# Twelve modulation vectors fetched or summed at other outputs in a fused two-block kernel

## The reference, cut to what matters

```python
mod = silu(c) @ w_ada + b_ada            # [1, 3072] a layer
shift, scale, gate = split(mod, 3)
h = rms_norm(x, g) * (1 + scale) + shift
x = x + gate * mixer(h)                  # the MLPs: x + 0.5 * gate * swiglu(h)
swiglu(x) = (silu(a) * b) @ w_down       # a, b = halves of x @ w_up
```

## Time and profile before

| | us |
|---|---|
| median of 3 runs | 1373.81 (1369.03 to 1379.53) |
| the profiled execution | 1375.45 |
| its span | 1373.7 |
| TensorE busy | 1204.4 (88%) |
| VectorE busy | 877.5 (64%) |
| DMA over the span | 160 GB/s |

### The profile page before, as it was taken

The page is one execution under the profiler, slowest core; times in us unless marked ns, Lnnn a source line. Parts: engine busy times, 40 slices in busy tenths (PEclk is TensorE's granted clock), DMA queues, the critical chain, the costliest instruction groups (busy, mean ns, idle before and its releaser), DMA issues. The chain is left out here.

```text
span 1373.7 us, 19952 instructions
## 1 busy us (share of the span) xinstructions
PE 1204.4 (88%) x7677; PEld 998.7 (73%) x7677; DVE 877.5 (64%) x1432; ACT 543.4 (40%) x962; POOL 286.1 (21%) x160
## 2 busy tenths in 40 slices
PE   4878896988896889999999878999798989999997
PEld 4665575766675667887877666889797967788886
DVE  4773697379856447865556785687556555555554
ACT  1232365242246353344453335334324243544443
POOL 0012042125421222441113323110313111000001
PEclk9989898899888799999999989789898989999999
DMA  7877155147745246976634335389000034555552
GB/s 267 282 244 230 62 184 169 62 155 262 241 138 170 92 138 219 323 225 199 192 118 152 112 123 154 120 261 338 1 4 2 4 102 143 169 184 184 184 169 76
DMA packets 143481, 221.62 MB, mean 161 GB/s; under 512 B 10823, under 2 KB 66715, under 8 KB 143259
## 3 DMA queue, kind: packets, MB, share of 16 engines
q1 hardware_dynamic: 140512, 216.37, 48.7%
q10 hardware_dynamic: 2875, 3.98, 0.8%
HBM read 219.27 MB, written 1.05 MB: 160 GB/s over the span
## 5 line engine op out<-in xcount | busy, mean ns | idle before, releaser
L532 PE MATMUL bank<-w_parts,lhs_hi 128*128 128x512 f32 (+2 forms) x960 | 399.3, 416 | 30.3 <-ACT w_parts L486 28.3
L486 ACT CAST w_parts<-ring 128x1024 fp32r<-128x1024 f32 (+2 forms) x288 | 288.7, 1032 | 280.3 <-PE bank L534 89.4
L534 PE MATMUL bank<-w_parts,lhs_lo 128*128 128x512 f32 (+2 forms) x960 | 391.7, 408 | 0.0
L491 DVE TENSOR_TENSOR w_parts<-ring,w_parts 128x1024 fp32r<-128x1024 f32 (+2 forms) x224 | 299.7, 1364 | 130.0 <-ACT w_parts L486 126.3
L547 PE MATMUL bank<-w_parts,lhs_hi 128*128 128x512 f32 (+2 forms) x960 | 276.2, 403 | 11.5 <-DVE w_parts L491 11.5
L532 PEld LDWEIGHTS bank<-w_parts,lhs_hi 128*128 128x128 f32 x960 | 191.3, 199 | 73.1 <-ACT w_parts L486 24.9
L491 POOL TENSOR_TENSOR w_parts<-ring,w_parts 128x1024 fp32r<-128x1024 f32 (+1 forms) x64 | 165.9, 2595 | 324.3 <-ACT w_parts L486 316.0
L547 PEld LDWEIGHTS bank<-w_parts,lhs_hi 128*128 128x128 f32 x960 | 183.5, 195 | 55.1 <-DVE w_parts L491 17.1
L534 PEld LDWEIGHTS bank<-w_parts,lhs_lo 128*128 128x128 f32 x960 | 191.0, 199 | 37.8
L662 DVE SCALAR_TENSOR_TENSOR ada_acc<-ring,c_act,ada_acc 128x512 f32<-128x512 f32 x203 | 176.6, 870 | 13.0 <-DMA ring<-in_ada_w 2.7
L609 PE MATMUL bank<-const,arena 128*128 128x128 f32 (+2 forms) x322 | 60.0, 340 | 34.9 <-DVE arena L1633 7.2
(11 more groups left out here) (347 smaller groups left out, 1531.2 us busy)
## 6 DMA issues: line engine op xcount, KB each, us to landing
ring<-in_w_ffn_up SPq DMA_DIRECT2D x176, 256.0 KB, 3.9
ring<-in_w_ada SPq DMA_DIRECT2D x72, 512.0 KB, 4.7
ring<-in_ada_w SPq DMA_DIRECT2D x48, 512.0 KB, 4.6
ring<-in_w_ffn_down SPq DMA_DIRECT2D x44, 512.0 KB, 4.4
ring<-in_w_in SPq DMA_DIRECT2D x44, 512.0 KB, 4.0
ring<-in_dil_w_in SPq DMA_DIRECT2D x32, 512.0 KB, 4.2
ring<-in_nsa_w_in SPq DMA_DIRECT2D x20, 512.0 KB, 4.6
ring<-in_w_in SPq DMA_DIRECT2D x20, 416.0 KB, 4.2
```

The costliest lines, as they stand in the source:

```text
L486: eng.copy(hi, raw).then_inc(hi_ready, 1)
L491: eng.tensor_tensor(lo, raw, hi.bitcast(F32), ALU.subtract).then_inc(lo_ready[who], 1)
L532: pe.matmul(b, x_hi, w, start=(k0 + k == 0), stop=False)
L534: mm = pe.matmul(b, x_lo, w, start=False, stop=False)
```

## The change

The vectors move down the stream:

| stage | before: vector after output | after |
|---|---|---|
| dilated | 12 to 16 after 1 to 5 | 12 to 15 after 1 to 4 |
| beside the attention | 17, 18 | 16, 17 |
| first MLP | 19 to 23 after 2 to 6 | 18 to 23 after 2 to 7 |
| z, gate outputs | 24, 25 after z; 26 to 29 after gate 0 to 3 | 24, 25 after z; 26, 27 after gate 0, 1 |
| last MLP | none | 28, 29 after 1, 2 |

TensorE's sums: in the dilated projections `ada_sum(10+j)` after output j (j = 2 to 5), so one output later than the fetch; 24 to 27 after z 1 and gate 0 to 2, also one later; in the first MLP 16+j after output j (j = 0 to 7), in the last 28 and 29 after outputs 1 and 2. From vector 12 on, the stream collects one vector less when it begins one.

```diff
+FFN1_ADAS = {j: 16 + j for j in range(8)}
+FFN2_ADAS = {1: 28, 2: 29}
 # first_stages
-        if j:
+        if 1 <= j < 5:
             s.append(ada(11 + j))
-    s.append(beside([...], range(17, 19), 1))
+    s.append(beside([...], range(16, 18), 1))
 # second_stages
-    ffn("ffn1", ..., {j: 17 + j for j in range(2, 7)})
+    ffn("ffn1", ..., {j: n for j, n in FFN1_ADAS.items() if n > 17})
-        s += [gemm("gate", j, ...), ada(26 + j)]
+        s.append(gemm("gate", j, ...))
+        if j < 2:
+            s.append(ada(26 + j))
-    ffn("ffn2", ..., {})
+    ffn("ffn2", ..., FFN2_ADAS)
 # stream_to
+                if who == "dve" and u == plan.outputs["gate", 3][1][0]:
+                    ada_collect_up_to(27)
-                        ada_collect_up_to(n)
+                        ada_collect_up_to(n if n < 12 else n - 1)
 # ffn_dve, after the multiplications of output j
-                if 0 <= j - 1 < len(adas):
+                if j - 1 in adas:
                     ada_collect_up_to(adas[j - 1] + 1)
 # ffn_pe, after output j
-                if j < len(adas):
+                if j in adas:
                     ada_sum(pe, adas[j])
 # dil_pe, after output j
-                    ada_sum(pe, 11 + j)
+                if j >= 2:
+                    ada_sum(pe, 10 + j)
-            pe.wait_ge(mod_ready, 17)
+            pe.wait_ge(mod_ready, 16)
 # mix_pe
-            ada_sum(pe, 24)
             ...
             gemm(pe, "z", 1, from_lhs, "norm3", 512)
-            ada_sum(pe, 25)
+            ada_sum(pe, 24)
             for j in range(4):
                 gemm(pe, "gate", j, from_lhs, "norm3", GATE_W)
-                ada_sum(pe, 26 + j)
+                if j < 3:
+                    ada_sum(pe, 25 + j)
```

More of the change, by code:

```diff
@@ L246, in first_stages @@
         s.append(gemm("dil", j, dw, 512 * j, 512, dve if j < 4 else act))
-        if j:
+        if 1 <= j < 5:
             s.append(ada(11 + j))
-    s.append(beside([(("dil", 6 + j), dw, 512 * (6 + j)) for j in range(2)], range(17, 19), 1))
+    s.append(beside([(("dil", 6 + j), dw, 512 * (6 + j)) for j in range(2)], range(16, 18), 1))
     s += [gemm("dil_out", j, do, 512 * j, 512, gated) for j in range(2)]
@@ L267, in ffn @@
             s.append(gemm(name + "_down", j, down, 512 * j, 512, gated, FC))
-    ffn("ffn1", A["w_ffn1_up_2"][0], A["w_ffn1_down_2"][0], {j: 17 + j for j in range(2, 7)})
+    ffn("ffn1", A["w_ffn1_up_2"][0], A["w_ffn1_down_2"][0], {j: n for j, n in FFN1_ADAS.items() if n > 17})
     w = A["w_in_2"][0]
@@ L279, in second_stages @@
     for j in range(4):
-        s += [gemm("gate", j, w, BA_AT + GATE_W * (j + 1), GATE_W, act), ada(26 + j)]
+        s.append(gemm("gate", j, w, BA_AT + GATE_W * (j + 1), GATE_W, act))
+        if j < 2:
+            s.append(ada(26 + j))
     for j in range(2):
@@ L286, in second_stages @@
         s.append(gemm("mix_out", j, A["w_out_2"][0], 512 * j, 512, gated))
-    ffn("ffn2", A["w_ffn2_up_2"][0], A["w_ffn2_down_2"][0], {})
+    ffn("ffn2", A["w_ffn2_up_2"][0], A["w_ffn2_down_2"][0], FFN2_ADAS)
     return s
@@ L1591, in dil_dve @@
                 rope_parts(dve, ("dil", j), lambda tt: gemm_bank("dil", j, tt)[:, :], 8)
-                if j:
-                    ada_collect_up_to(11 + j)
+                if j >= 2:
+                    ada_collect_up_to(10 + j)
             stream_ahead("dve", "dil", 4)
             read_turns("dve", "dil_q", lambda b: dil_qT[:, 2 * b:2 * b + 2, :].rearrange("p c t -> p (c t)"), range(4))
-            stream_to("dve", plan.outputs["ada", 16][1][-1])
+            stream_to("dve", plan.outputs["dil", 5][1][-1])
+            ada_collect_up_to(15)
             read_turns("dve", "dil_k", lambda b: dil_kT[:, 2 * b:2 * b + 2, :].rearrange("p c t -> p (c t)"), range(4))
-            ada_collect_up_to(17)
+            ada_collect_up_to(16)
             def weigh(grp):
@@ L1605, in weigh @@
                                   weight.broadcast_to([P, TT, HP, DH]), ALU.mult).then_inc(dil_att.pv_read, 1)
-            dil_att.dve(dve, link, weigh, lambda i: ada_beside(17, i),
+            dil_att.dve(dve, link, weigh, lambda i: ada_beside(16, i),
                         lambda i: stream_ahead("dve", "dil_out", 0, -0.5))
@@ L1703, in build, with ffn_dve @@
         FFN_AT = {"ffn1": 0, "ffn2": 1}
-        def ffn_dve(dve, name, layer, adas=()):
+        def ffn_dve(dve, name, layer, adas):
             base = 2 * FFN_OUTS * FFN_AT[name]
@@ L1720, in ffn_dve @@
                     turned_left_dve(dve, name + "_h", [j - 1], up_pair)
-            if adas:
-                ada_collect_up_to(adas[-1] + 1)
             residual_half_dve(dve, layer)
@@ L1733, in ffn_act, with ffn_pe @@
                     turned_left_act(act, name + "_h", [j - 1], up_pair)
-        def ffn_pe(pe, name, norm, adas=()):
+        def ffn_pe(pe, name, norm, adas):
             for j in range(FFN_OUTS + 1):
@@ L1947, in mix_dve @@
             stream_ahead("dve", "a_out", 0, 0)
-            ada_collect_up_to(30)
+            ada_collect_up_to(28)
             for j in range(2):
@@ L2224, in delta_pe @@
             await_turns_read(pe, "v", range(4))
-            pe.wait_ge(mod_ready, 30)
+            pe.wait_ge(mod_ready, 28)
             for r in range(ROUNDS):
@@ L2499, in second_dve @@
         def second_dve(dve, link):
-            ffn_dve(dve, "ffn1", 2, range(17, 24))
+            ffn_dve(dve, "ffn1", 2, FFN1_ADAS)
             norm_dve(dve, 2, link)
@@ L2503, in second_dve @@
             norm_dve(dve, 3, link)
-            ffn_dve(dve, "ffn2", 4)
+            ffn_dve(dve, "ffn2", 4, FFN2_ADAS)
             final_dve(dve, link)
@@ L2529, in second_pe @@
         def second_pe(pe):
-            ffn_pe(pe, "ffn1", "norm2", range(17, 24))
+            ffn_pe(pe, "ffn1", "norm2", FFN1_ADAS)
             into_norm(pe, 2, from_up, "ffn1_h", FC)
             mix_pe(pe)
-            ffn_pe(pe, "ffn2", "norm4")
+            ffn_pe(pe, "ffn2", "norm4", FFN2_ADAS)
             for _ in gemm_steps(pe, "ffn2_down", 1, from_up, "ffn2_h", 512, FC, by_tile=4):
```

## The result

The changed kernel takes **1396.82 us** (median of 4 runs, 1389.94 to 1402.41) against 1372.46 for the kernel before beside it (4 runs, 1369.03 to 1379.53). The ratio is 1.017, 95% interval 1.010 to 1.023: slower, by 24 us. Its profiled execution took 1399.59 us, with a span of 1397.8 and a mean clock of 0.924 (before: 1373.7 and 0.925).

A forecast was written before the change was run, and what follows sets the result against it. VectorE was taken to bound the dilated projections, TensorE the first MLP, with TensorE's rhythm setting the last. Dilated -7, mixer -7, first MLP +17 and last MLP +8 gave +11, so 1384.8, rounded to 1385; range 1374 to 1397.

The forecast's parts named there:

- The dilated projections, -7: Dilated projections: waits for vectors go and the attention starts earlier, 7 us gained, bounds -3 and -9.
- The text's own sign of being wrong: Dilated projections: if low parts before 360 come earlier, VectorE was not the bound and the prediction is wrong.
- The first MLP, +17, bounds 9 to 21: First MLP: late collection makes TensorE wait after outputs 1 to 7, with clock drops and one more sum; 17 us lost.
- 14.9 an output: First MLP: VectorE's own chain with the collection, the limit if the clock doesn't drop, against 13.8 for TensorE.
- each stall pulls the clock down: First MLP: each of six new stalls lowers the clock as the one at 519.28 did, 6 x 1.6 = 9.6 us.
- The rival of VectorE and GpSimd, 1394, chance 0.2: First MLP: GpSimd subtractions hold VectorE up just before five of six new waits, +9 us, total 1394; chance 0.2.
- GpSimd is done by then: First MLP: argument against the collision rival, that a slower rhythm gives GpSimd its high parts earlier.
- The mixer, -7, bounds -4.6 and -8: Hybrid mixer: a wait and its clock drop go (5.8), two gate vectors leave (3.4), a low part comes late (1.2).
- nothing, or up to 1 us: Mixer: cost of vector 24's sum leaving the v turns, where copies set the pace, through a longer cold stretch.
- a risk of up to 2: Mixer: if gate 2's weights are still late, up to 2 of the 7 us gained are lost.
- The last MLP, +8: Last MLP: two gate sums (3.4), one wait for vector 28's collection (1.62 and 1.3), a drop of 1.6; bounds +5 and +10.
- The faster rival, 1366, chance 0.1: MLPs: if VectorE has collected the vector when an output's last matmul ends, the stalls don't appear; 1366, chance 0.1.

The follow-up runs named there:

- experiment 1: Kernel before, with one edit: for vectors 19 to 23 the last waiting vector is collected behind the two multiplications; 1395.6 us, ratio 1.017 to before.
- experiment 2: Changed kernel with the call that collects a vector put ahead of the stream and the multiplications in both MLPs; 1361.8 us, ratio 0.992 to before.
- experiment 7: Changed kernel with both MLPs' vectors summed one output later on TensorE, collection still behind the multiplications; 1361.8 us, ratio 0.988 to before.
- Experiment 3: Changed kernel with GpSimd's share of the first MLP's low parts given to VectorE; 1379.9 us, ratio 1.006 to before.
- experiment 5: Changed kernel with the collection ahead of the multiplications, and vector 24's sum back ahead of the v turns; 1364.0 us, ratio 0.991 to before.
- experiment 8: Changed kernel with the collection ahead of the multiplications, and GpSimd's first-MLP low parts given to VectorE; 1355.7 us, ratio 0.985 to before.
- experiment 10: Changed kernel with the collection ahead, no low parts on GpSimd but for two pairs of outputs beside the attentions; 1342.9 us, ratio 0.976 to before.

## Why the prediction came out as it did

The direction, the place and the cause, the late collection, were right, as experiments 1, 2 and 7 show. The time is 1396.8 where 1385 was forecast. It lies inside the range by 0.2 us, which is luck: the first MLP's term missed by 13.6 and lies outside its own bounds. Slower by over 1% had a chance of 0.38, less than the 0.56 of staying within 1%. Nearly all of the gap is this one term.

- **The dilated projections, -7: right.** The two profiles say -9.4, but over all kernels with GpSimd in this stage the old form takes 94.8, 96.4, 96.7 and 96.8 and the new one 86.9 to 89.8 (eight kernels, median 89.0): -7.5. The waits for vectors are gone, and TensorE waits for low parts in their place (2.10, 2.25, 3.77), as it must where VectorE is the bound. The text's own sign of being wrong, a low part that comes earlier before 360, did show: the one at 359.60 began 2.3 us earlier (361.40, in a run that was 4.1 late). But it ran beside a GpSimd subtraction (361.06 to 363.71), took 3.38 us instead of 1.21, and ended only 0.15 earlier. So nothing was gained ahead of 360.8, as the text said.
- **The first MLP, +17, bounds 9 to 21: too small, by 13.6.** The sum of 1.7 is right to within what can be read. The waits are the term that was mis-sized: put at 7.6, they came to 22.8 - 1.62 - 0.34 = 20.8. The step that failed is the one that reckoned each wait from silu, multiplication and collection alone, and made "14.9 an output" VectorE's limit. It took one pass of VectorE from the rhythm of before, whose first step took 0.48 us, and moved it into the new one. There, where the clock has dropped, the sum and the turn run at 1.2 GHz, so `up_lo` starts 2.86 us after the sum instead of 2.27. And GpSimd's two subtractions fall onto a vector's steps or a low part: the first step takes 2.62 on average. The chain became 17 to 19.7.

  Experiment 3 took GpSimd out, and the six new waits came to 11.6 against the text's 7.9 (before it took off the 0.34). So 9.6 of their 21.2 go with the subtractions. The other 3.6 stay, in a kernel in which VectorE has two low parts more an output.

  The drops of the clock were put at six times 1.6, and cost 8.1 in all (30.6 less the new waits and the sum), but "each stall pulls the clock down" did not hold. From sum to sum, less the wait at the end, the outputs behind 528.13, 545.37, 562.75, 580.62 and 597.59 take 14.4, 14.3, 15.9, 12.8 and 15.1 us; at 2.4 GHz it is 12.7, or 13.5 with a gate's sum. So there was no drop at 580.62, and the others cost 1.6 to 3.2; behind 617.24 it is another 1.7. That is nearly 10 for five drops, less the one of 1.6 that the kernel before had at 519.28 and the changed one has not. That the total is near 9.6 is luck.

  The pass that was taken was a lucky one even before. In that kernel, from 521 to 588, two of the five first steps (there L656) took 0.48 us and three 2.0 to 2.6, so the mean stands at 1.61:

```profile
L656 DVE TENSOR_SCALAR ada_acc<-ring,c_act 128x512 f32<-128x512 f32 x5 | 8.1, 1613 | 0.0
```

- **The rival of VectorE and GpSimd, 1394, chance 0.2: right in the cause, in its condition and nearly in the time.** It was to decide when GpSimd works as an output ends, and at five of six ends it does, so the argument against it ("GpSimd is done by then") was false. It also named a low part or a vector's step that runs into a subtraction just before the wait, which is what stands ahead of these five. It was wrong on the scales, which it named first: the collections themselves took 0.15 to 0.68 us, and the scales even lost the 2.17 that they had before. And it reckoned one block of 1.9 us where VectorE was held up 4.2 us an output. The rule cited from the Trainium skill (SBUF - State Buffer, section SBUF: two separate sides) should have been applied to the low parts and the vector's steps, not to the collections alone. In the traces, steps and low parts take up to 2.2 us more beside a subtraction, while shifts, which read a bank, take 0.15 even where a subtraction runs beside them (at 523.5 and 538.2 in the kernel before), as that rule has it.
- **The mixer, -7, bounds -4.6 and -8: too hopeful.** Seven kernels with the new form, GpSimd's share in place and no further edit here take 326.0 to 330.7 (median 327.8); three with the old form 331.0 to 332.5: about -3. The wait of 2.87 is gone. But the term "nothing, or up to 1 us" for vector 24's sum was too low: the sum had filled a wait. Now TensorE idles 5.61 ahead of the v turns, z 1 starts 9.2 us after z 0's end instead of 8.3, and its first matmuls take 0.63 us. From z 0's end to the sum behind z 1 it is 21.9 us against 19.9, so the term came to 2.0. The low part of gate output 1 is late by 1.43, as forecast (1.2), and the weights behind it by 1.10. The 1.10 is the late weights that the text cost at nothing, and named as a risk of up to 2. Against its terms these three are 1.0, 0.2 and 1.1 of the 4 us; the rest is not shown, and experiment 5, made for the first, did not decide.
- **The last MLP, +8: about right in size, with one term too many.** It is +6.4 from the last wait for a low part in its output 0 (1180.57 and 1198.32) to the last turn: one wait of 2.5 us (put at 1.6 + 1.3) and two sums of 1.8. The drop of 1.6 did not come, though this wait was longer than the one it was read from. With the collection ahead (experiment 2) 3.6 of the 6.4 remain, the two sums.
- **The faster rival, 1366, chance 0.1,** said what would happen if VectorE had collected a vector before its output ends. Experiment 2 builds just that, 1361.8 (on a chip where before took 1373.1).

## What to carry to other kernels

Moving a step later doesn't move its wait: ask what the waiting instruction waits for and where that is produced in the other engine's program order. Here two lines' order was worth 25 us, and the order of one call decided between 1.7% slower and 0.8% faster. And a duration read from the trace holds for its neighbours of that moment: before a chain is moved to a new rhythm, reckon it with the durations of the unlucky case too, for a small helper on another engine can cost more than it saves. Ask also what each engine will be doing at the moment when the new wait begins: here a helper was at work at five of six such moments.

## What was unexpected of the hardware

- A GpSimd subtraction of 2.4 to 2.7 us saves VectorE 1.2 us and costs it up to 2.1 (a first step of 0.48 takes 2.62, a pair of steps of 1.54 takes 3.55). All subtractions taken off GpSimd outside the attentions made the old kernel 1.3% and the new one (by experiments 8 and 10, besides the first MLP's) another 0.9% faster, though VectorE was the bound of the dilated projections and got more low parts to do.
- A stall's length alone did not tell whether the clock drops. A wait of 1.62 us was followed by 1.2 GHz in the kernel before (519.28), and waits of 1.62, 1.98 and 2.51 us in the changed kernel were not.
- The same 290 us of instructions took 289.9 to 296.7 us from execution to execution, each on one core, not always of the same chip.
